# Norm weight as a scale per partition on the gathered expert rows, with strided row blocks for TensorE

## What is computed

```python
x = x + merged @ w_out
x = x + hier_moe(rms_norm(x, g_ffn), w_group, b_group, w_expert, ...)

def hier_moe(h, ...):                      # cut
    g_prob = softmax(t @ w_group + b_group)            # 4 groups, best one taken
    e_prob = softmax((t @ w_expert + b_expert)[group]) # 8 experts in it, best two taken
    top_w  = g_gate * top_p / sum(top_p)
    for e in range(32):
        hid = silu(t @ w_gate[e]) * (t @ w_up[e])      # 1024 -> 512
        out += combine[:, e] * (hid @ w_down[e])       # 512 -> 1024
```

## Time and profile before

| | us |
|---|---|
| median of 3 runs (2520.52 to 2522.07) | 2520.83 |
| profiled execution, its own time | 2520.5 |
| its span | 2518.6 |
| PE busy | 2313.8 (92%) |
| DVE busy | 1485.1 (59%) |
| ACT busy | 1156.6 (46%) |
| POOL busy | 424.3 (17%) |

### The profile page before, as it was taken

The page is one execution under the profiler, slowest core; times in us unless marked ns, Lnnn a source line. Parts: engine busy times, 40 slices in busy tenths (PEclk is TensorE's granted clock), DMA queues, the critical chain, the costliest instruction groups (busy, mean ns, idle before and its releaser), DMA issues.

```text
span 2518.6 us, 29086 instructions
## 1 busy us (share of the span) xinstructions
PE 2313.8 (92%) x9901; PEld 1650.1 (66%) x9901; DVE 1485.1 (59%) x1501; ACT 1156.6 (46%) x1174; POOL 424.3 (17%) x151
## 2 busy tenths in 40 slices
PE   6899995999999999989987889999899978889997
PEld 4344544566566565558877766788688777667886
DVE  6966337888888888855545434455455464424554
ACT  4122414666666766643324546433343244464332
POOL 2640000000000000010005456300100053555000
PEclk8899997999999999999988999999999998999999
DMA  5234252999999999945543243555355432434652
GB/s 211 67 117 131 87 178 103 354 368 366 363 363 360 369 361 360 383 156 182 183 133 102 88 132 132 168 184 183 118 196 187 136 126 74 134 117 142 201 184 91
DMA packets 166450, 496.80 MB, mean 197 GB/s; under 512 B 10272, under 2 KB 21792, under 8 KB 136400
## 3 DMA queue, kind: packets, MB, share of 16 engines
q1 hardware_dynamic: 164528, 491.70, 55.2%
q10 hardware_dynamic: 1616, 3.24, 0.4%
q0 software_dynamic: 208, 0.59, 0.1%
HBM read 494.45 MB, written 1.05 MB: 197 GB/s over the span
## 4 chain that ended last, share of the span: by engine, by line
PE 66%; issue 14%; DVE 10%; POOL 6%; ACT 3%; DVEq 0%; DMA 0%; ACTq 0%; POOLq 0%
PE ps L967 11%; PE ps L968 11%; PE ps L969 11%; PE ps L1347 9%; PE ps L1018 6%; POOL w_lo L3041 6%; PE ps L1328 5%; PE ps L1332 5%; PE ps L1038 1%; PE ps L1316 1%; PE ps L1109 1%; PE ps L1385 1%; DVE W_r L2704 1%; ACT w_hi L1790 1%; PE ps L1364 1%
## 5 line engine op out<-in xcount | busy, mean ns | idle before, releaser
L3041 POOL TENSOR_TENSOR w_lo<-raw,w_hi 128x2048 fp32r<-128x2048 f32 x72 | 335.1, 4672 | 1599.8 <-ACT w_hi L1592 1404.5
L1592 ACT ACTIVATE w_hi<-raw 128x2048 fp32r<-128x2048 f32 (+1 forms) x204 | 378.9, 1865 | 459.2 <-PE ps L969 414.2
L967 PE MATMUL ps<-w_hi,a_hi 128*128 128x512 f32 (+1 forms) x1216 | 476.4, 392 | 54.7 <-POOL w_lo L3041 29.9
L968 PE MATMUL ps<-w_lo,a_hi 128*128 128x512 f32 (+1 forms) x1216 | 466.9, 384 | 0.0
L969 PE MATMUL ps<-w_hi,a_lo 128*128 128x512 f32 (+1 forms) x1216 | 465.3, 383 | 0.0
L2065 DVE TENSOR_TENSOR w_lo<-raw,w_hi 128x2048 fp32r<-128x2048 f32 (+1 forms) x132 | 293.1, 2227 | 264.4 <-ACT w_hi L1592 257.2
L967 PEld LDWEIGHTS ps<-w_hi,a_hi 128*128 128x128 f32 x1216 | 236.1, 194 | 105.9 <-POOL w_lo L3041 32.6
L969 PEld LDWEIGHTS ps<-w_hi,a_lo 128*128 128x128 f32 x1216 | 235.3, 194 | 44.4
L968 PEld LDWEIGHTS ps<-w_lo,a_hi 128*128 128x128 f32 x1216 | 236.2, 194 | 40.8
L1328 PE MATMUL ps<-w_hi,W_r 128*128 128x512 f32 x468 | 190.8, 408 | 5.4 <-DVE w_lo L2704 4.7
L967 PE MATMUL ps<-w_hi,y_hi 128*128 128x512 f32 x384 | 156.8, 408 | 18.4 <-DVEq L2530 18.4
(11 more groups left out here) (404 smaller groups left out, 3747.6 us busy)
## 6 DMA issues: line engine op xcount, KB each, us to landing
raw<-in_w_in SPq DMA_DIRECT2D x56, 1024.0 KB, 5.1
raw<-in_ffn_w_gate SPq DMA_DIRECT2D x44, 1024.0 KB, 5.1
raw<-in_ffn_w_up SPq DMA_DIRECT2D x44, 1024.0 KB, 5.1
raw<-in_ffn_w_down SPq DMA_DIRECT2D x40, 1024.0 KB, 5.0
raw<-in_w_up SPq DMA_DIRECT2D x30, 1024.0 KB, 7.9
raw<-in_w_gate SPq DMA_DIRECT2D x30, 1024.0 KB, 7.1
lo_f<-in_w_up SPq DMA_DIRECT2D x30, 1024.0 KB, 8.1
lo_f<-in_w_down SPq DMA_DIRECT2D x29, 1024.0 KB, 7.6
```

The costliest lines, as they stand in the source:

```text
L967: pe.matmul(dst, a_h, b_h, start=first, stop=False, **kw)
L968: pe.matmul(dst, a_h, b_l, start=False, stop=False, **kw)
L1592: act.activation(E.view(w_hi, name), E.view(raw, name), ACT.Copy).then_inc(hi_split, 1)
L3041: pool.tensor_tensor(E.view(w_lo, name), E.view(raw, name), E.view(w_hi, name).bitcast(F32), ALU.subtract)\
```

## The change

- `gain_row`, its matmuls and copies, and the normed rows in `xn` are gone. A small table `gain_f` (128 partitions by 8) holds the norm weight in the order of the row blocks; eight small DMAs on ACT's queue bring it in.
- ACT rounds x times the root directly (`scale=` a column), DVE's difference uses `scalar_tensor_tensor` on x. The rows stay in their natural order.
- A gather takes its block with a step of four floats from `h_rows`, and adds the hi and the lo product in the same 256 columns of PSUM.
- The evacuation of a gather is two operations: ACT rounds the 256 columns times `gain_f` (`gathered_hi`), then DVE takes the difference (`gathered`), and DVE's frees the bank.
- ACT rounds the first two matrices (four units) before it waits for the residual; POOL takes their four differences. The wait for the first square is for the first half of the tokens alone.
- The memset of `hid_e` moves ahead of the wait for the root.

```diff
-            for h in range(2):
-                dst = bank(("gain_row", h))
-                for k in range(4):
-                    m = pe.matmul(dst[:, k * P:k * P + P], gain["f"][:, 4 * h + k:4 * h + k + 1].broadcast_to([P, P]), ident, ...
-                fill(m, ("gain_row", h))
...
-                        m = pe.matmul(dst[:, half * SEQ:half * SEQ + SEQ], h_rows[half][:, t, kb * P:kb * P + P], pick[:, t, :],
-                                      start=half == 0 and t == 0, stop=half == 1 and t == 1, skip_group_check=True)
+                        at = slice(512 * (kb // 4) + kb % 4, 512 * (kb // 4) + 512, 4)
+                        m = pe.matmul(dst[:, 0:SEQ], h_rows[half][:, t, at], pick[:, t, :], start=half == 0 and t == 0,
+                                      stop=half == 1 and t == 1, skip_group_check=True)
...
-                        pe.wait_ge(done["gathered_act"], nth("gathered_act", (k, 1)))
+                        pe.wait_ge(done["gathered"], nth("gathered", (k, 1)))
...
+            at_gain = P + 2 * KB
+            gain_src = A["packed"][:, at_gain:at_gain + KB].rearrange("(b k) (h a) -> a b h k", k=4, a=4)
+                for a in range(4):
+                    for h in range(2):
+                        act.dma_start(gain_f[32 * a:32 * a + 32, 4 * h:4 * h + 4], gain_src[a][:, h]).then_inc(gain_loaded, 16)
...
-            act.wait_ge(done["residual"], nth("residual", ("wo", 1, 1)))
-            stats("f", x_sb, junk_f)
+            for name in FIRST_TILES[0:2]:
+                for half in range(2):
+                    expert_rounded(name, half)
             for t in range(2):
-                act.wait_ge(done["normed"], nth("normed", t))
-                act.activation(h_rows[0][:, t], xn[:, t], ACT.Copy).then_inc(done["row_hi"], 1)
+                act.wait_ge(done["residual"], nth("residual", ("wo", 1, t)))
+                act.activation(junk_f, x_sb[:, t, :], ACT.Square, accum_out=st_ss[:, t:t + 1]).then_inc(scalar_step, 1)
+                act.wait_ge(scalar_step, step.next())
+            inverse_root("f", st_ss, r_of["f"], D)
+            for t in range(2):
+                act.activation(h_rows[0][:, t], x_sb[:, t], ACT.Copy, scale=r_of["f"][:, t:t + 1]).then_inc(done["row_hi"], 1)
...
-            def gathered_copy(name, kb, group):
+            def gathered_hi(name, event, kb, group):
                 act.wait_ge(bank_filled[bank_of[name]], fills(name))
-                act.activation(packed_rows[group][:, kb].rearrange("p q (h s) -> p h q s", h=2),
-                               psum(name).rearrange("p (h q s) -> p h q s", h=2, q=GROUP_TILES), ACT.Copy)...
+                act.activation(packed_rows[group][:, kb, :, 0:SLOTS], psum(name)[:, 0:SEQ].rearrange("p (q s) -> p q s", s=SLOTS),
+                               ACT.Copy, scale=gain_f[:, kb:kb + 1]).then_inc(done["gathered_hi"], 1)
...
             def gathered(name, event, kb, group):
-                evacuate(name, packed_rows[group][:, kb].rearrange("p q (h s) -> p h q s", h=2), ...
+                dve.wait_ge(done["gathered_hi"], nth("gathered_hi", event))
+                rows = packed_rows[group][:, kb]
+                stt(out=rows[:, :, SLOTS:P], in0=psum(name)[:, 0:SEQ].rearrange("p (q s) -> p q s", s=SLOTS),
+                    scalar=gain_f[:, kb:kb + 1], in1=rows[:, :, 0:SLOTS].bitcast(F32), op0=ALU.mult, op1=ALU.subtract)\
+                    .then_inc(bank_freed[bank_of[name]], 1)
...
(DVE's period: gather 0 after the copy of the transposes, gather 1 after hidden_rows)
+                if gathers:
+                    gathered(("G", k, 0), (k, 0), kb, group)
                 dve.wait_ge(done["scattered"], marks["scattered"].number(k, regs))
...
                     hidden_rows(k, column(tile + 1))
+                if gathers:
+                    gathered(("G", k, 1), (k, 1), kb + 1, group)
...
(DVE before the loop)
-                for kb in range(0, KB, 2):
+                for kb in range(KB):
                     gathered(("G", "first", 0, kb), ("first", 0, kb), kb, 0)
-                expert_lower(("g", "first"), 0)
-                expert_lower(("g", "first"), 1)
                 spots()
-                expert_lower(("u", "first"), 0)
-                expert_lower(("u", "first"), 1)
...
(POOL)
+            for name in FIRST_TILES[0:2]:
+                for half in range(2):
+                    u = (name, half)
+                    pool.wait_ge(expert_hi, E.split_number(u) + 1)
+                    pool.tensor_tensor(E.expert_raw(u)[1], E.expert_raw(u)[0], E.expert_hi(u).bitcast(F32), ALU.subtract)\
+                        .then_inc(expert_lo, 1)
             pool.wait_ge(done["residual"], nth("residual", ("wo", 1, 1)))
```

More of the change, by code:

```diff
@@ L345, in plan @@
         fill(("G", "first", 0, kb), kb % 4)
-    mark("gathered", *(("first", 0, kb) for kb in range(0, KB, 2)))
-    mark("gathered_act", *(("first", 0, kb) for kb in range(1, KB, 2)))
+    for signal in ("gathered_hi", "gathered"):
+        mark(signal, *(("first", 0, kb) for kb in range(KB)))
     expert_unit(("g", "first")); expert_unit(("u", "first")); expert_unit(("g", "second"))
@@ L351, in plan @@
         fill(("G", "first", 1, kb), 2 + kb)
-        mark("gathered_act", ("first", 1, kb))
+        mark("gathered_hi", ("first", 1, kb)); mark("gathered", ("first", 1, kb))
     fill(("g", "second"), 0)
@@ L608, in bass_hybrid_moe_then_swa_gla @@
         expert_at, one_col = tile_at[:, 0:EXPERTS], iota[:, 1:2]
-        gain_row = area(o, D); o += D
+        gain_f = area(o, KB); o += KB
         rt = area(o, 2, 36); o += 72
@@ L1422, in experts @@
                 fill(m, "slot_weights")
-                pe.wait_ge(done["gathered"], nth("gathered", ("first", 0, KB - 2)))
-                pe.wait_ge(done["gathered_act"], nth("gathered_act", ("first", 0, KB - 1)))
+                pe.wait_ge(done["gathered"], nth("gathered", ("first", 0, KB - 1)))
                 expert_rows(("g", "first"), 0, 0)
@@ L1769, in _ @@
             act.dma_start(iota, A["head_rows"][0:SEQ].partition_broadcast(P)).then_inc(tables_loaded, 16)
+            at_gain = P + 2 * KB
+            gain_src = A["packed"][:, at_gain:at_gain + KB].rearrange("(b k) (h a) -> a b h k", k=4, a=4)
+            with nc.allow_non_contiguous_dma(reason="the gain in the order of the expert rows"):
+                for a in range(4):
+                    for h in range(2):
+                        act.dma_start(gain_f[32 * a:32 * a + 32, 4 * h:4 * h + 4], gain_src[a][:, h]).then_inc(gain_loaded, 16)
             for hh in range(2):
@@ L1850, in period @@
                 if gathers:
-                    gathered_copy(("G", k, 0), kb, group)
+                    gathered_hi(("G", k, 0), (k, 0), kb, group)
                 if gate:
@@ L1858, in period @@
                 if gathers:
-                    gathered_copy(("G", k, 1), kb + 1, group)
+                    gathered_hi(("G", k, 1), (k, 1), kb + 1, group)
                 if up:
@@ L1870, in experts @@
                 route()
[L1871 to L1877, removed]
+                act.wait_ge(gain_loaded, 128)
+                for kb in range(KB):
+                    gathered_hi(("G", "first", 0, kb), ("first", 0, kb), kb, 0)
                 lower_half(("first", "g"), bank_of[("g", "first")], fills(("g", "first")), low_g)
@@ L1881, in experts @@
                 for kb in range(2):
-                    gathered_copy(("G", "first", 1, kb), kb, 1)
+                    gathered_hi(("G", "first", 1, kb), ("first", 1, kb), kb, 1)
                 gated("first")
@@ L2488, in _ @@
                     dve.sem_inc(done["gained"], 1)
[L2490 to L2502, removed]
-                    ins = stt(out=xn[:, t, part].rearrange("p (k s) -> p k s", k=4), in0=by_part(x_sb[:, t, part]),
-                              scalar=r_of["f"][:, t:t + 1], in1=gain_row[:, part].rearrange("p (k s) -> p k s", k=4),
-                              op0=ALU.mult, op1=ALU.mult)
-                    if h == 0:
-                        ins.then_inc(vector_step, 1)
-                        dve.wait_ge(vector_step, step.next())
-                ins.then_inc(done["normed"], 1)
-                dve.wait_ge(done["normed"], nth("normed", t))
+            dve.memset(hid_e[SLOTS:P], 0.0).then_inc(vector_step, 1)
+            dve.wait_ge(vector_step, step.next())
             def hidden(k, dst, gate_, w, weight):
@@ L2532, in route @@
             def route():
+                dve.wait_ge(done["rstd"], nth("rstd", "f"))
                 for t in range(2):
@@ L2593, in route @@
                     dve.wait_ge(done["row_hi"], nth("row_hi", t))
-                    tt(h_rows[1][:, t], xn[:, t], h_rows[0][:, t].bitcast(F32), ALU.subtract).then_inc(done["row_lo"], 1)
+                    stt(out=h_rows[1][:, t], in0=x_sb[:, t], scalar=r_of["f"][:, t:t + 1], in1=h_rows[0][:, t].bitcast(F32),
+                        op0=ALU.mult, op1=ALU.subtract).then_inc(done["row_lo"], 1)
```

(8 more changed lines are left out.)

21 lines of the change are left out of this document (8 added, 13 removed).

## The result

| | before | after |
|---|---|---|
| median, us | 2521.4 (2519.9 to 2525.3) | 2562.9 (2557.5 to 2565.9, 6 runs) |
| ratio | | 1.0167, 95% interval 1.0154 to 1.0181 |
| span of the traced execution | 2518.6 | 2561.3 |

What follows compares the result with a forecast made beforehand. PE was taken to bound the expert tiles, DVE's chain the stretch between projection and loop. -7.2 + 28 + 1 + 0.8 + 0.8 = +23.4 on 2520.5 us gave 2544 us; 8-in-10 range 2513 to 2556.

Steps and rivals of the forecast that it cites:

- The strided load: Gathers in the expert tiles: each load takes 0.23 us, 0.11 more; 0.8 per tile, +28 us over 35 tiles; 43 in 100.
- The 28.8 us: Expert loop: +28 us for the strided loads in 35 tiles and +0.8 for the waits for `pick`.
- the waits for `pick`: Every fourth tile, PE waits longer for DVE's later `pick`: +3.8 us over 8 waits, only 0.8 if PE's tile grows.
- pieces of 16 bytes: Gather loads: 128 floats at step four are 128 pieces at 1.8 ns each, so 0.23 us per load.
- hidden: Rival for the gathers: a strided load stays under 0.12 us and costs nothing; 2517 us, 24 in 100.
- read twice: Rival for the gathers: the load reads its source twice, +0.34 us each, 2.6 per tile; 2609 us, 15 in 100.
- DVE and ACT in a tile: Expert tiles: DVE gains two operations of 0.48 us, delaying only `pick` at every fourth tile; +3.8 us, 0 to +8.
- Bank 0: Loop: freed at 585.1, wanted by the gate rows at 586.62, so not late; PE waiting there would show the prediction wrong.
- Before the loop: Between projection and expert loop: five items on the chain, -7.2 us in sum, bounds -5 to -9.
- The norm and the differences: Before the loop: routing-sum evacuation moves earlier by 3.3 us; two differences ahead of `spots` go to POOL, -4.4 us.
- partly in the shadow: First group's gathers before the loop: strided loads run partly at the lower clock, partly under DVE's evacuation; +1 us.
- POOL's cover: Before the loop: POOL's four differences, 18.7 us, run from 347 to 366 beside the projection; first use past 406.

Runs made afterwards that it cites:

- a_shift16: The changed kernel with 16 unused semaphore increments at the start of DVE's program, so that its loop lies later: 2543.7 us, ratio 1.0097.
- a_packed_shift16: a_packed with 16 unused semaphore increments at the start of DVE's program: 2520.2 us, ratio 0.9992.
- a_fill: The changed kernel with block-order rows, six fewer DVE increments per tile, earlier `pick`, and 22 unused matmuls ahead of the routing matmuls: 2505.7 us, ratio 0.9945.
- b_shift4: The kernel before with 4 unused semaphore increments at the start of DVE's program: 2541.8 us, ratio 1.0080.
- a_packed: The changed kernel, but ACT and DVE write the rows in block order, so the gathers' loads are packed: 2542.2 us, ratio 1.0074.

## Why the prediction was wrong

With these runs the loop's 46.6 us part cleanly, each term the difference of two loops above, one trace each: 17.6 for where the loop lies (697.0 - 679.4), 25.4 for the strided loads (679.4 - 654.0), 3.6 for the longer DVE part in the loop (654.0 - 650.4).

1. **The strided load: right, in mechanism and size.** Forecast 0.23 us per load and 0.8 per tile; measured 0.23 and 0.81. The 28.8 us with the waits for `pick` measure 29.0 (25.4 + 3.6). The argument by pieces of 16 bytes held, and "hidden" and "read twice" are both out. Why a packed load takes 140 ns in one place and 188 in the other, on which the second rested, no run here shows. Of the two readings of the Trainium skill's rule, the one in Advanced Engine Details and Errata, SBUF Cachelines (two accesses on a line for full speed) agrees with the 0.23; the one in SBUF — State Buffer, under Door 1, that counts four floats as free doesn't.
2. **"DVE and ACT in a tile" failed.** It priced the added work of DVE by the time of its operations (two of 0.48 us): 3.8 us, with 0 to 8 as bounds. Their instructions it put at nothing, without a reason. Waits and increments are instructions too: the trip grew from 261 to 302, its end moved from position 828 to 870, past 830, and its start lies before 575. That costs 17.6 us, nearly the whole of the miss in the loop (46.6 - 28.8 = 17.8). Against a_shift16 these are 11.4 us more idle time of PE (21.0 against 9.6) and 6.2 us in which PE does the same matmuls for longer (busy 676.0 against 669.7), at the lower clock. Two of the 17.6 lie in the low stretch ahead of the first branch back, which none of the four other kernels that stall has, so its tie to the place of the loop isn't shown: some 15.6 belong to the branches. That DVE's loop lay at 568 to 828 could have been read from the trace of before; that an edge comes behind 830, two places on, only the later runs showed.
3. **The waits for `pick`: right.** Alone, DVE's later `pick` costs 3.6 us of loop, and its waits grow by 11.6 - 7.8 = 3.8 (a_packed_shift16; I had 3.8); beside a longer tile it is 8.8 - 7.8 = 1.0 (0.8). Bank 0, the prediction's other sign, made PE wait once in the changed kernel, 0.9 us behind the first branch back, and never in a_shift16.
4. **Before the loop: -3.4 instead of -7.2 + 1.8.** The norm and the differences went as said. Two sizes didn't, 2 us together. The 32 routing matmuls took 4.77 us instead of 3.76: the granted clock fell from 1.00 to 0.50 at 382.6 us, 2.5 us into them, while in the kernel before it was 1.00 to their end. I had costed the removed norm-weight matmuls at nothing, though PE now stands for 2.29 us ahead of the routing; a_fill shows that filling this pause can give back 1.9 us on them (3.66 against 5.60). But in b_shift4, which has no such pause, they took 4.81 and the clock fell at 382.6 us all the same, so for the change itself this cause stays open. And the eight gathers follow each other at 0.93 us, four strided loads each, so DVE's evacuation takes 8.8 us and not the 7.0 of its own operations and 1 for the loads: I had laid the strided loads "partly in the shadow" of DVE, and it is the reverse.
5. **POOL's cover held:** 351.4 to 369.4, on the old scale 347.3 to 365.3, against the forecast 347 to 366, long before the first use.

Over the whole: 2544 + 17.6 for the place of the loop, + 2 for the first stretch, gives 2563.6, and 2562.9 was measured (the +4.1 ahead of the change and the -4.6 behind it nearly cancel, which is luck). The change's loss is a layout cost, which is the change's own, and a placement cost, which it met by chance: with both taken away (a_packed_shift16) it is as fast as before, 0.9992.

## What to carry over

With a stationary operand at a step of 16 bytes, matmuls of 256 columns follow each other at 0.23 us instead of 0.12 at the full clock, and where PE sets the time all of that is paid, so let the engine that writes the rows anyway do the reordering, as a_packed does. Count an engine's instructions in a hardware loop, waits and increments among them, and look at where the loop begins: here four more instructions outside it cost 21 us. Where long gaps of "issue" and packets on an instruction queue follow each branch back, shift the loop before changing it.

## What the hardware showed

- At each branch back of a misplaced DVE loop, 4.4 to 7.5 us pass between the branch's record and DVE's next one, a part of them while DVE still works on its last operation. A second gap of some 4 us follows a few instructions on, and the tile is 3 to 9 us longer. At a well placed loop's branch it is 0.24 to 0.35 us to the next record.
- LDWEIGHTS of 128x128 in the short form: 188 ns packed, 312 to 330 ns at a step of 16 bytes; the pace of the matmuls of 256 columns behind them 0.12 and 0.23 us. Ahead of the loop of the changed kernel a gather's four took 0.93 to 0.95 us both at a granted clock of 0.50 (401.17 to 403.05 us) and at 1.00 (403.95 to 406.75): this pace hardly follows TensorE's clock. So the strided load costs little at the lower clock, where packed pairs of these matmuls start 0.42 to 0.43 us apart (a_packed_shift16) and strided ones 0.47 to 0.48.
- The same 32 small matmuls ahead of the routing took from 4.77 to 6.41 us in eight kernels in which PE had stood for 2.29 us before them, and 3.66, 3.76 (four times) and 4.81 in six with at most 0.50. The pause isn't all: in b_shift4, the one of the six with 4.81, the granted clock fell at the same 382.6 us as in the changed kernel. What sets that time no run here shows.
